# Down projections of two feed-forward blocks in seven half-width products instead of eight

## The reference, cut to what matters

```python
def _conv_ffn(h, w_up, conv_w, conv_b, w_down):
    u, v = jnp.split(h @ w_up, 2, axis=-1)          # 1024 -> 2 x 2816
    ...
    return (jax.nn.silu(uc) * v) @ w_down           # 2816 -> 1024
...
for l in range(DEPTH):                              # DEPTH = 2
    ...
    y = _conv_ffn(h, ffn_w_up[l], ffn_conv_w[l], ffn_conv_b[l], ffn_w_down[l])
    x = _layer_norm(ALPHA * x + g2 * y, ln_g[l, 1], ln_b[l, 1])
```

## Time and profile before

| | us |
|---|---|
| time before, median of 3 (2510.96 to 2514.28) | 2511.22 |
| the profiled execution, own time | 2517.16 |
| its span | 2515.9 |
| down projection, layer 0 (window) | 157.5 |
| down projection, layer 1 (window) | 157.6 |
| mean granted clock of TensorE in the span | 0.972 |

### The profile page before, as it was taken

The page is one execution under the profiler, slowest core; times in us unless marked ns, Lnnn a source line. Parts: engine busy times, 40 slices in busy tenths (PEclk is TensorE's granted clock), DMA queues, the critical chain, the costliest instruction groups (busy, mean ns, idle before and its releaser), DMA issues.

```text
span 2515.9 us, 38126 instructions
## 1 busy us (share of the span) xinstructions
PE 2370.7 (94%) x16538; PEld 1595.0 (63%) x16538; DVE 1503.7 (60%) x2608; ACT 630.2 (25%) x1292; POOL 87.9 (3%) x157
## 2 busy tenths in 40 slices
PE   7988889999997999999999999999997999999997
PEld 3675548888443688874455676676765654546973
DVE  3884368887456878862127969779787123232443
ACT  1323331111002311110133354544543312101111
POOL 2000000000100000000000000000000000000000
PEclk9999999999998999999999999999998999999999
DMA  8232235555542133342112101001000212111102
GB/s 326 99 103 75 78 123 169 181 176 182 180 158 94 67 126 138 130 149 89 46 50 115 37 20 37 15 26 37 3 35 18 84 50 84 51 50 67 34 18 100
DMA packets 41063, 227.87 MB, mean 91 GB/s; under 512 B 4609, under 2 KB 4737, under 8 KB 24641
## 3 DMA queue, kind: packets, MB, share of 16 engines
q1 hardware_dynamic: 20304, 140.55, 15.4%
q0 software_dynamic: 20016, 82.79, 9.5%
q10 hardware_dynamic: 576, 2.11, 0.2%
HBM read 219.14 MB, written 6.29 MB: 90 GB/s over the span
## 4 chain that ended last, share of the span: by engine, by line
PE 90%; DVE 6%; ACT 2%; issue 1%; DMA 1%; SPq 0%; DVEq 0%; ACTq 0%
PE ps L658 21%; PE ps L303 19%; PE ps L2062 10%; PE ps L3162 3%; PE ps L1843 3%; PE ps L818 2%; PE ps L435 2%; PE ps L3351 2%; PE ps L1494 2%; PE ps L2072 2%; PE ps L2081 2%; PE ps L2469 1%; PE ps L2782 1%; PE ps L2750 1%; PE ps L2769 1%
## 5 line engine op out<-in xcount | busy, mean ns | idle before, releaser
L303 PE MATMUL ps<-G,ring 128*128 128x512 f32 x704 | 303.5, 592 | 0.0
L2062 PE MATMUL ps<-H,ring 128*128 128x256 f32 (+1 forms) x832 | 271.4, 487 | 5.4 <-ACT LW L2281 2.6
L658 PE MATMUL ps<-right_sums,left_sums 128*128 128x256 f32 x1056 | 242.6, 379 | 0.0
L303 PEld LDWEIGHTS ps<-G,ring 128*128 128x128 f32 x704 | 133.7, 190 | 166.6 <-issue 166.5
L2062 PEld LDWEIGHTS ps<-H,ring 128*128 128x128 f32 x832 | 157.4, 190 | 113.0 <-issue 92.8
L658 PEld LDWEIGHTS ps<-right_sums,left_sums 128*128 128x128 f32 x1056 | 200.6, 190 | 27.3
L303 PE MATMUL ps<-H,ring 128*128 128x512 f32 (+1 forms) x480 | 181.5, 535 | 0.9 <-DVE ls_tmp L3029 0.9
L658 PE MATMUL ps<-H,ring 128*128 128x256 f32 x704 | 164.9, 386 | 12.6 <-ACT H L601 12.6
L658 PEld LDWEIGHTS ps<-H,ring 128*128 128x128 f32 x704 | 135.2, 193 | 35.4 <-issue 12.8
L303 PEld LDWEIGHTS ps<-H,ring 128*128 128x128 f32 x480 | 91.1, 190 | 88.3 <-issue 84.9
L472 DVE SCALAR_TENSOR_TENSOR R<-ps,mod,XA 128x512 f32<-128x512 f32 x24 | 18.0, 750 | 205.5 <-PE ps L303 188.8
(11 more groups left out here) (550 smaller groups left out, 4195.4 us busy)
## 6 DMA issues: line engine op xcount, KB each, us to landing
ada_late<-ada_rest POOLq DMA_DIRECT2D x104, 512.0 KB, 3.6
ring<-w_up SPq DMA_DIRECT2D x44, 1024.0 KB, 4.8
ring<-w_down SPq DMA_DIRECT2D x16, 1408.0 KB, 5.9
ring<-od_in SPq DMA_DIRECT2D x16, 1024.0 KB, 4.9
ring<-ev_in SPq DMA_DIRECT2D x15, 1024.0 KB, 4.8
ada_early<-ada_rest POOLq DMA_DIRECT2D x24, 512.0 KB, 4.4
ada_first_sb<-ada_first SPq DMA_DIRECT2D x8, 1024.0 KB, 16.3
ring<-ab_in SPq DMA_DIRECT2D x7, 1024.0 KB, 6.0
```

The lines of the kernel that those rows point to most:

```text
L303: mm = pe.matmul(k.ps[:, (n % deep) * nb + b, 0:tn], wv[:, kk, a * P:(a + 1) * P], rhs[:, kk, t0:t0 + tn], start=(kk == 0), stop=(kk == kt ...
L658: return pe.matmul(product(k, n, j), lhsT[:, i, :], rhs[:, i, :], start=(i == 0), stop=(i == 3))
L2062: mm = pe.matmul(k.ps[:, bank + b, 0:tn], wv[:, kk, (i % 2) * P:(i % 2 + 1) * P], k.H[:, kk, t0:t0 + tn], start=(kk == 0), stop=(kk == DT ...
```

## The change

Both down projections are done like the up projection, in seven half-width products. The depth of 22 tiles is 11 pairs, cut in groups h of 4, 4 and 3 pairs (`DEEP`); a round is one group of one pair of output tiles, and `DOWN` gives the order of the 12 rounds per layer. A round with 4 pairs has 28 matmuls of 128x256, one with 3 pairs 21, in steps of 2, 2, 2 and 1 products. The rounds use the two halves of PSUM in turn. Sums of weight blocks ("left", four operations of 128 x 128 per pair count) are made by GpSimd each round, and so are the sums of `G` blocks ("right") for group 0; those of groups 1 and 2 are made by VectorE between rounds. Each round's result is added to the rows at once (`down_evac_dve`), so VectorE has eight operations a round in place of one a tile. ScalarE copies one product a round out of PSUM. The sum and the square of tile 6 move behind the last product. LATE becomes 3. Of layer 0's ada tiles 8 move from its down projection to that of layer 1, which has 13 in place of 5. The ada tiles now follow the round's evacuation. The load of the `rw_consts` table and its use move to the end of the down projection of layer 1 and behind the pre-norm.

```diff
+DEEP = ((0, 4), (4, 4), (8, 3))
+DOWN = [(0, 0), (0, 1), (0, 2), (0, 3), (1, 0), (1, 1), (2, 0), (2, 1), (1, 2), (1, 3), (2, 2), (2, 3)]
-EARLY, LATE = 3, 4
+EARLY, LATE = 3, 3
+ADA_DOWN = [[range(N_ADA[0] + 44 + a, N_ADA[0] + 44 + b) for a, b in ((0, 2), (2, 4), (4, 5), (5, 7), (7, 8), (8, 10), (10, 11), (11, 12), (12, 13), (13, 14), (14, 16), (16, 17))],
+            [range(N_ADA[0] + 83 + a, N_ADA[0] + 83 + b) for a, b in ((0, 1), (1, 2), (2, 3), (3, 4), (4, 6), (6, 8), (8, 9), (9, 10), (10, 11), (11, 12), (12, 13), (13, 13))]]
+def ffn_pool(k, l, first):
+    ...
+    issued(ADA_UP[l][10].stop)
+    first_right_pool(k, l)
+    issued(ADA_UP[l][FT - 3].stop)
+    for it in range(ND):
+        down_left_pool(k, l, it)
+        issued(ADA_UP[l][FT - 1].stop if it == 0 else ADA_DOWN[l][it - 1].stop)
+def down_left_pool(k, l, it):
+    ...
+    g.wait_ge(*k.when("slab", k.slab(f"w_down{l}_{h}", q)))
+    if it:
+        g.wait_ge(*(k.when("down products", l, it - 2, 3) if it >= 2 else k.when("products", l, FT - 1, 3)))
+    g.tensor_tensor(S[1], A[1, 0], A[1, 1], ALU.add).then_inc(*k.says(POOL))
+    g.wait_ge(*k.now(POOL))
+    g.tensor_tensor(S[2], S[1], A[0, 0], ALU.subtract).then_inc(*k.says(POOL))
+    g.tensor_tensor(S[3], A[0, 0], A[1, 0], ALU.subtract).then_inc(*k.says(POOL))
+    g.wait_ge(*k.now(POOL))
+    g.tensor_tensor(S[4], A[0, 1], S[2], ALU.subtract).then_inc(*k.says(POOL, "down left", l, it))
 def ffn_down_pe(k, l):
+    for it, (h, q) in enumerate(DOWN):
+        ...
+        pe.wait_ge(*k.when("slab", g))
+        pe.wait_ge(*k.when("ffn g", l, (7, 15, FT - 1)[h]))
+        pe.wait_ge(*(k.when("down done", l, it - 2) if it >= 2 else k.when("ffn v", l, FT - 2 + it)))
+        for e, terms in enumerate(steps):
+            if e == 1:
+                pe.wait_ge(*k.when("down left", l, it))
+                pe.wait_ge(*k.when("down right", l, h))
+            ...
+            if e == 3 and it == ND - 1:
+                pe.wait_ge(*k.when("down done", l, it - 1))
+                pe.wait_ge(*k.when(st, "upper"))
+                pe.matmul(k.ps[:, DOWN_MEAN, :], ones, k.ln_mu[:], start=True, stop=False)
+                pe.wait_ge(*k.when(st, "squares added"))
+                for j in range(2):
+                    pe.matmul(k.ps[:, DOWN_SQUARE, :], ones, sq[:, j, :], start=(j == 0), stop=False)
+            for left, right, j in terms:
+                for i in range(ni):
+                    mm = pe.matmul(product(k, it, j), left[:, i, :], right[:, i, :], start=(i == 0), stop=(i == ni - 1))
+            mm.then_inc(*k.says(PE, "down products", l, it, e))
+def down_evac_dve(k, l, it, middle=None):
+    ...
+    v.wait_ge(*k.when("down first", l, it))
+    v.scalar_tensor_tensor(R[:, t0, 0:HALF], first, g0, base[:, t0, 0:HALF], ALU.mult, ALU.add).then_inc(*k.says(DVE))
+    v.wait_ge(*k.when("down products", l, it, 1))
+    settled(k, v.tensor_tensor(X[:, 0, :], first, product(k, it, 6), ALU.add), "down first used", l, it)
+    settled(k, v.tensor_tensor(X[:, 1, :], X[:, 0, :], product(k, it, 5), ALU.add))
+    settled(k, v.scalar_tensor_tensor(R[:, t0, HALF:T], X[:, 1, :], g0, base[:, t0, HALF:T], ALU.mult, ALU.add))
+    if middle:
+        middle()
+    v.wait_ge(*k.when("down products", l, it, 2))
+    v.scalar_tensor_tensor(halves(R[:, t0, :]), seconds, g0, halves(R[:, t0, :]), ALU.mult, ALU.add).then_inc(*k.says(DVE, "down tile", l, t0, h))
+    settled(k, v.scalar_tensor_tensor(halves(R[:, t1, :]), X, g1, halves(base[:, t1, :]), ALU.mult, ALU.add))
+    settled(k, v.scalar_tensor_tensor(halves(R[:, t1, :]), over_two(product(k, it, 7)), g1, halves(R[:, t1, :]), ALU.mult, ALU.add))
+    v.wait_ge(*k.when("down products", l, it, 3))
+    v.scalar_tensor_tensor(R[:, t1, 0:HALF], product(k, it, 4), g1, R[:, t1, 0:HALF], ALU.mult, ALU.add).then_inc(*k.says(DVE, "down done", l, it))
 def ffn_down_dve(k, l):
+    for it in range(ND):
+        down_evac_dve(k, l, it, squares_joined if it == ND - 1 else None)
+        if it < 4:
+            down_right_dve(k, l, 1, it)
+        elif it == 4:
+            for j in range(2):
+                down_right_dve(k, l, 2, j)
+        elif it == 5:
+            for j in range(2, 4):
+                down_right_dve(k, l, 2, j)
+        ...
+        for j in ADA_DOWN[l][it]:
+            ada_tile_dve(k, j)
```

More of the change, by code:

```diff
@@ new lines, in down_right_dve @@
+def down_right_dve(k, l, h, j):
+    v = k.nc.vector
+    B, R = down_right(k, DOWN.index((h, 0)))
+    if j == 0:
+        if h == 1:
+            v.wait_ge(*k.when("products", l, FT - 1, 3))
+        else:
+            v.wait_ge(*k.when("down products", l, 3, 3))
+        v.tensor_tensor(R[1], B[0, 1], B[0, 0], ALU.subtract).then_inc(*k.says(DVE))
+        v.wait_ge(*k.now(DVE))
+    if j == 1:
+        v.tensor_tensor(R[2], B[1, 1], R[1], ALU.subtract).then_inc(*k.says(DVE))
+    if j == 2:
+        v.tensor_tensor(R[3], B[1, 1], B[0, 1], ALU.subtract).then_inc(*k.says(DVE))
+        v.wait_ge(*k.now(DVE))
+    if j == 3:
+        v.tensor_tensor(R[4], B[1, 0], R[2], ALU.subtract).then_inc(*k.says(DVE, "down right", l, h))
@@ new lines, in ffn_down_pe @@
+def ffn_down_pe(k, l):
+    pe, st, ones, sq = k.nc.tensor, ("norm", l, 1), k.c("ones"), k.down_sq
+    for it, (h, q) in enumerate(DOWN):
+        g, ni = k.slab(f"w_down{l}_{h}", q), down_pairs(it)[1]
+        A, S = down_left(k, l, it)
+        B, R = down_right(k, it)
+        steps = (((A[0, 0], B[0, 0], 1), (A[0, 1], B[1, 0], 2)), ((S[2], R[2], 6), (S[1], R[1], 5)), ((S[4], B[1, 1], 3), (S[3], R[3], 7)), ((A[1, 1], R[4], 4),))
+        pe.wait_ge(*k.when("slab", g))
[5 more added lines that the diff above has]
+                pe.wait_ge(*k.when("down right", l, h))
+            if e == 2 and l == 1 and it == 2:
+                pe.wait_ge(*k.when("down done", l, 1))
+                context_sum_pe(k)
+            if e == 3 and l == 1 and it == 3:
+                pe.wait_ge(*k.when("context rstd"))
+            if e == 3 and it == 8:
+                pe.wait_ge(*k.when(st, "half"))
+                for j in range(2):
+                    mm = pe.matmul(k.ps[:, DOWN_C, :], ones, sq[:, j, :], start=(j == 0), stop=(j == 1))
+                mm.then_inc(*k.says(PE, st, "half sum"))
+            if e == 3 and it == 9:
+                pe.wait_ge(*k.when(st, "half mean"))
+                if l == 0:
+                    pe.wait_ge(*k.when("down done", l, 8))
+                    bias_sum_pe(k)
+            if e == 3 and it == 10 and l == 0:
+                pe.wait_ge(*k.when("bias read"))
+            if e == 3 and it == ND - 1:
[9 more added lines that the diff above has]
+            mm.then_inc(*k.says(PE, "down products", l, it, e))
+        k.mark(PE, "slab used", g)
+    for n in (6, 7):
+        pe.wait_ge(*k.when("down tile", l, n))
+        mm = pe.matmul(k.ps[:, DOWN_MEAN, :], ones, k.R[:, n, :], start=False, stop=(n == 7))
+        if n == 7:
+            mm.then_inc(*k.says(PE, st, "sum"))
+        pe.wait_ge(*k.when(st, "square", n))
+        mm = pe.matmul(k.ps[:, DOWN_SQUARE, :], ones, sq[:, n, :], start=False, stop=(n == 7))
+        if n == 7:
+            mm.then_inc(*k.says(PE, st, "variance"))
@@ new lines, in down_act @@
+def down_act(k, l, late=None):
+    a, st, sq, R = k.nc.scalar, ("norm", l, 1), k.down_sq, k.R
+    for it in range(ND):
+        a.wait_ge(*k.when("down products", l, it, 0))
+        if it >= 2:
+            a.wait_ge(*k.when("down first used", l, it - 2))
+        a.copy(k.DP[:, it % 2, :], product(k, it, 1)).then_inc(*k.says(ACTE, "down first", l, it))
+        if l == 1 and it == 0:
+            context_squares_act(k)
+        if l == 1 and it == 2:
+            context_rstd_act(k)
+        if l == 1 and it == 4:
+            context_h_act(k)
+        if it == 9:
+            for j in range(2):
+                a.wait_ge(*k.when(st, "shifted", j))
+                a.activation(sq[:, pair(j), :], R[:, pair(j), :], ACT.Square).then_inc(*k.says(ACTE, st, "square", j))
+    a.wait_ge(*k.when("down tile", l, 5))
+    a.activation(sq[:, 4:6, :], R[:, 4:6, :], ACT.Square).then_inc(*k.says(ACTE, st, "square", 5))
+    for n in (6, 7):
+        if late and n == 7:
+            late(k)
+        a.wait_ge(*k.when("down tile", l, n))
+        a.activation(sq[:, n, :], R[:, n, :], ACT.Square).then_inc(*k.says(ACTE, st, "square", n))
@@ L3020, in rw_consts_pool @@
     g = k.nc.gpsimd
-    g.wait_ge(*k.when("pooled", 0))
+    g.wait_ge(*k.when("down products", 1, ND - 1, 1))
     g.dma_start(k.rwc[:], k.dram["rw_consts"]).then_inc(*k.lands("rw_consts_in", "rw consts"))
```

153 lines of the change are left out of this document (107 added, 46 removed).

## The result

| | before | after |
|---|---|---|
| median (all runs) in us | 2511.09 (2510.52 to 2514.28, 4 runs) | 2497.97 (2495.48 to 2501.06, 4 runs) |
| ratio after / before, 95% interval | | 0.9942 [0.9928, 0.9956] |
| profiled execution: own time / span | 2517.16 / 2515.9 | 2495.48 / 2494.1 |
| first product to the end of the last, layer 0 | 157.3 | 143.7 |
| the same, layer 1 | 157.5 | 146.9 |

The kernel is faster by 13 us in the medians (by the ratio 14.6), where 30.4 were forecast (2480.8, range 2474 to 2495). The time lies above the range. The lines of the profile have moved: what was `L303`, `L658`, `L2081` is now `L307`, `L683`, `L2302`; the new products are `L905`, the evacuation is `L958` to `L972`, GpSimd's sums of weights are `L823` to `L828`, the right sums of VectorE `L853` to `L861`.

A forecast was written before the change was run, and what follows sets the result against it. Number and width of PE's matmuls were taken to bound the down projections. 36.1 + 2.2 saved, less stalls of 2 x 0.8, 2 x 1.9, 2.3 and 0.2, gave 30.4 us: 2511.2 to 2480.8, range 2474 to 2495.

The forecast's parts named there:

- Products and pitch: Both down projections: 704 matmul instructions at 0.429 us become 1232 at 0.2159, 302.1 to 266.0 us, saving 36.1.
- twice 1.7: End of each layer: tile 6's sum and square leave the product stream, 4 instructions x 0.429 = 1.7 us less per layer.
- Waits of layer 0's down projection: PE stalls: 0.8 us for group 2's right sums, 1.9 at left 7, 0.2 at left 10 and 11, 2.3 for joined squares.
- left 7: GpSimd's left sums for round 7, queued behind ada transfers: ready at 14.3, due at 12.4; stall 1.9 us, both layers.
- the joined squares: Last round, layer 0: VectorE finishes them at 10.9 us after round 10, PE wants them at 8.6; stall 2.3. Layer 1 in time.
- The mean's chain: Behind layer 0's products: the mean can start 3.4 us after the last product, 1.2 later than before; net gain 0.5.
- GpSimd's price: GpSimd adding two tiles of 512 columns in left sums: taken as 1.49 us, its one-operand row; 2.98 from above.
- Against it: Evidence against mutual exclusion: a VectorE two-operand operation overlapping a one-operand GpSimd operation (1.49 us) took its usual 1.28 us.
- the rival in which the two engines shut each other out: Two-SBUF-operand operations wait for each other; ten tight left sums cost 7 us: 2488, or 2493 with clock loss; chance 0.26.
- the right sums of group 0 delay only ada transfers: Up projection, rounds 11 and 12: about 12 us of GpSimd work, costing PE nothing because three buffers cover the transfers.
- The clock behind layer 1: PE's wait behind layer 1 shrinks to 1.6 us, which may avoid half clock and win 1.9 us.
- The price at 2.2 us per GpSimd operation: Left sums in the down projections slower: loss about 20 us, time 2494; chance 0.07 for 2 to 2.7 us per operation.

The follow-up runs named there:

- Runs 2 and 3: Changed kernel with GpSimd's four left-sum operations as memsets (run 2, 2489.06 us) or one-operand operations (run 3, 2491.76 us), the sums left out.
- left_memset: Changed kernel with GpSimd's four left-sum operations replaced by memsets that read nothing, sums left out of the result: 2489.06 us, ratio 0.9901 to before.
- left_one_operand: Changed kernel with GpSimd's four left-sum operations replaced by operations on one tile (times 0.5), sums left out: 2491.76 us, ratio 0.9908 to before.
- before_padded: Kernel before with 73 more instructions in TensorE's stream, all already satisfied waits: 2518.3 us, ratio 1.0022 to before.
- before_again: Kernel before, unchanged, run and profiled once more: 2513.42 us, ratio 0.9995 to its twin.

## Why the prediction was wrong

- *Products and pitch: right.* 36.6 us less PE time for 36.1. Without waits the window of a layer is 138.4 us (143.7 - 5.24 and 146.9 - 6.87 - 1.6 of half clock), so both layers give 38.0 us before waits, where the prediction's terms give 39.5 (36.1 and twice 1.7). The 1.5 us between them I didn't trace.
- *Waits of layer 0's down projection: right* in place, kind and size, 5.24 us for 5.2. The prediction's queue for left 7 and its sum for the joined squares hold. *The mean's chain* behind layer 0 was right too: from the end of the products to the first matmul on `pooled` 11.48 us before and 12.61 after, 1.1 for 1.2.
- *GpSimd's price: near.* Forecast 1.49 us for 512 columns, measured 1.26 to 1.28 undisturbed and 1.28 to 1.46 in the mean. The Trainium skill's 4497 ns for 2048 columns (GPSIMD Engine Reference, section 3.1) gave an estimate of 1.15, below every one of these.
- *The first step that failed: "Against it"*, the price given to the rival in which the two engines shut each other out. It was laid aside on one overlap in which GpSimd had a single operand, and the kernel's work has two. Runs 2 and 3 show the taking of turns: with the reads gone VectorE's operations in layer 1 lose 16.8 us of length, with one operand nearly as much, and the times fall by 7 to 9 and by 4.6 us (2496.38 - 2491.76). What it cost beyond the forecast in the down projections is 5.8 us (5.24 + 6.87 + 1.6 of half clock, for 7.9). It fell where the prediction had put "in time": the joined squares of layer 1 (2.70 for 0), the right sums there (2.73 for 0.8), and the half clock behind them, 1.6 us.
- *The second step that failed*, by the same mechanism: that the right sums of group 0 delay only ada transfers. The term was put at nothing, and they cost 2.7 us, since VectorE's sums of weights in those rounds take 2.72 to 3.24 us each for 0.69, and PE waits 1.27 and 1.40 us. With it the mechanism's price is 8.5 us; the rival's own working had 7 (2488), up to 12.7 with the clock (2493). That is about right, though its terms (ten left sums) are not where the time went.
- The Trainium skill (SBUF — State Buffer, "Who interferes with whom") has a VectorE instruction with two SBUF inputs contend with a GpSimd one that reads SBUF, and not with one that only writes. Runs after and left_memset agree with it (1534 against 744 ns). In left_one_operand, where GpSimd reads, the same form stays at 742 ns; other forms grow a little (`L1003` 1371 for 1218 ns), so there the rule holds weakly.
- *What no case had:* the scan stage, 5.5 us (before_padded) to 6.7 (the passes of before and after), lost by where its code lies. The prediction took everything outside of the changed stages as unchanged.
- *The clock behind layer 1*, which the prediction held possible as a gain, is none: before_again has it at full speed too.
- *A sum.* The price at 2.2 us per GpSimd operation, 2494, doesn't follow from its terms: 2511.2 - (38.3 - 3.9 - 20) is 2496.8. It set the high end of the range, 2495, which was too low by the prediction's own working.

The terms together: 38.0 - 1.1 for the mean's chain - 13.7 of waits and half clock in the down projections - 2.7 in the up projections - 5.5 to 6.7 in the scan stage leave a gain of 13.8 to 15.0 us. Measured are 14.6 and 17.6 by the two ratios; the difference is of the size by which executions scatter. Without the scan stage's loss the gain would be 20.5 and the time 2490.7, inside of the range. So of the missing 15.4 to 16.6 us, 8.5 are a mechanism that was named and given too little weight, and 5.5 to 6.7 one that was not thought of. The chance of 0.26 for the first should have been above one half: the row against it didn't show the case at hand.

## What to carry to other kernels

When work goes to GpSimd beside a busy VectorE, count how many of their operations have all operands in SBUF and lie in the same microseconds, and give both their longer lengths; a row in which they overlap speaks only for its own kinds of operands. Then place VectorE's optional work behind, not in front of, what PE waits for next. A piece of work put on an idle engine is not free for the neighbour: ask of each what the other does in the same microseconds, in the stages too that the change seems to leave alone. When a change moves the number of instructions of an engine, compare the "issue" waits of stages that it doesn't touch, and try the kernel with some satisfied waits more, before believing a difference of a few tenths of a per cent.
